# RMS pre-norms moved from the inputs of the weight units to their outputs, with the modulation column sums at other places, in a kernel of two transformer stacks

## The reference

```
for layer in range(2):
    shift, scale, gate = split(c @ mod_w[layer, 0] + mod_b[layer, 0], 3)
    h = rms_norm(x, norm_w[layer, 0, 0]) * (1 + scale) + shift
    y = mixer_ab(h) if layer == 0 else mixer_cd(h)     # attention mixers
    x = x + gate * rms_norm(y, norm_w[layer, 0, 1])
    shift, scale, gate = split(c @ mod_w[layer, 1] + mod_b[layer, 1], 3)
    h = rms_norm(x, norm_w[layer, 1, 0]) * (1 + scale) + shift
    y = (silu(h @ Wg) * (h @ Wu)) @ Wd                 # 2816 hidden
    x = x + gate * rms_norm(y, norm_w[layer, 1, 1])
# second stack: same form with shift, scale and gate from c_2 @ w_ada,
# x = x + gate * y (no norm of y), a mixer of block attention and a token
# MLP, an FFN with a 3-tap convolution over the tokens of h @ w_up, and a
# last rms_norm
```

## Time and profile before

| | us |
|---|---|
| median of 3 runs | 1102.88 |
| lowest, highest | 1096.81, 1103.98 |
| profiled execution | 1099.16 |
| its span, first to last instruction | 1097.4 |
| TensorE busy | 1040.6 (95%) |
| VectorE busy | 759.1 (69%) |
| ScalarE busy | 520.1 (47%) |

### The profile page before, as it was taken

One profiled execution on the slowest core, in us unless ns is written; L12 is line 12 of the kernel. 1 busy time (PEld: TensorE's weight loads), 2 busy tenths in 40 slices (PEclk: granted clock), 3 DMA queues, 4 the chain that ended last, 5 costly groups with the idle time before them and its releaser, 6 DMA issues.

```text
span 1097.4 us, 21157 instructions
## 1 busy us (share of the span) xinstructions
PE 1040.6 (95%) x8292; PEld 997.8 (91%) x8292; DVE 759.1 (69%) x1161; ACT 520.1 (47%) x906; POOL 4.6 (0%) x14
## 2 busy tenths in 40 slices
PE   5999879999999999999999999999977999999995
PEld 5998669999999999889999999999956999999995
DVE  3757875777777656685577777766764577777785
ACT  2445763544444455464454444446532355555552
POOL 0100000000000000000000000000000000000000
PEclk9999999999999999999999999999965999999999
DMA  9966664488888728604198898854520525545651
GB/s 353 321 208 229 237 215 171 153 307 308 313 294 307 256 74 300 199 1 137 64 315 297 307 299 307 287 211 146 181 96 1 170 85 211 186 172 185 224 186 39
DMA packets 62837, 229.12 MB, mean 209 GB/s; under 512 B 7058, under 2 KB 7314, under 8 KB 62388
## 3 DMA queue, kind: packets, MB, share of 16 engines
q1 hardware_dynamic: 61988, 225.59, 59.1%
q0 software_dynamic: 640, 2.10, 0.8%
q10 hardware_dynamic: 144, 0.52, 0.1%
HBM read 226.62 MB, written 1.57 MB: 208 GB/s over the span
## 4 chain that ended last, share of the span: by engine, by line
PE 81%; DVE 9%; ACT 5%; issue 2%; DMA 2%; SPq 0%; DVEq 0%; ACTq 0%
PE bank L1647 21%; PE bank L1649 21%; PE bank L1648 21%; PE bank L1673 3%; PE bank L1664 2%; DVE acc L549 2%; PE bank L1665 2%; DVE otok L1132 2%; ACT wH L726 1%; PE bank L1777 1%; PE bank L2273 1%; DVE hL L1127 1%; DVE wL L1080 1%; DMA modbuf<-in_mod_w 1%; PE bank L1747 1%
## 5 line engine op out<-in xcount | busy, mean ns | idle before, releaser
L1647 PE MATMUL bank<-hH,wH 128*128 128x256 f32 x1576 | 453.5, 288 | 6.5 <-DVE hL L1127 2.6
L1648 PE MATMUL bank<-hL,wH 128*128 128x256 f32 x1576 | 446.8, 284 | 0.0
L1649 PE MATMUL bank<-hH,wL 128*128 128x256 f32 x1576 | 446.7, 283 | 0.0
L1080 DVE TENSOR_TENSOR wL<-raw,wH 128x1024 fp32r<-128x1024 f32 x273 | 325.9, 1221 | 132.8 <-ACT wH L726 132.7
L1647 PEld LDWEIGHTS bank<-hH,wH 128*128 128x128 f32 x1576 | 303.2, 192 | 13.8 <-issue 8.3
L726 ACT ACTIVATE wH<-raw 128x1024 fp32r<-128x1024 f32 x273 | 273.4, 1049 | 78.1 <-PE bank L1649 59.1
L1648 PEld LDWEIGHTS bank<-hL,wH 128*128 128x128 f32 x1576 | 303.5, 193 | 0.1
L1649 PEld LDWEIGHTS bank<-hH,wL 128*128 128x128 f32 x1576 | 303.2, 192 | 0.0
L1647 PE MATMUL bank<-aH,wH 128*128 128x256 f32 x560 | 160.3, 286 | 2.1 <-DVE aL L1265 2.1
L1648 PE MATMUL bank<-aL,wH 128*128 128x256 f32 x560 | 159.7, 285 | 0.0
L1649 PE MATMUL bank<-aH,wL 128*128 128x256 f32 x560 | 159.6, 285 | 0.0
(11 more groups left out here) (295 smaller groups left out, 1123.2 us busy)
## 6 DMA issues: line engine op xcount, KB each, us to landing
raw<-in_weights SPq DMA_DIRECT2D x273, 512.0 KB, 4.9
modbuf<-in_mod_w SPq DMA_DIRECT2D x83, 512.0 KB, 5.1
modbuf<-in_w_ada SPq DMA_DIRECT2D x48, 512.0 KB, 5.2
strips<-bias_table POOLq DMA_DIRECT2D x8, 256.0 KB, 6.2
otok<-in_cmp_w SPq DMA_DIRECT2D x4, 512.0 KB, 8.6
raw<-in_mod_w SPq DMA_DIRECT2D x2, 512.0 KB, 4.9
otok<-in_mod_w SPq DMA_DIRECT2D x2, 512.0 KB, 11.3
sn<-in_mod_w SPq DMA_DIRECT2D x2, 512.0 KB, 12.8
```

The costliest lines, as they stand in the source:

```text
L1080: V.tensor_tensor(wL[:, slot, :], raw[:, slot, :], wH[:, slot, :].bitcast(F32), ALU.subtract).then_inc(lo_ready[c], 1)
L1647: mm(out, lhs_h, rhs_h, start=start, stop=False, skip_group_check=True)
L1648: mm(out, lhs_h, rhs_l, start=False, stop=False, skip_group_check=True)
L1649: return mm(out, lhs_l, rhs_h, start=False, stop=stop, skip_group_check=True)
```

## The change

1. For norms A1 to A5 the rows that go into the units are x*(1+scale)*w, without 1/rms (`raw_high` on ScalarE, `raw_low` on VectorE). hH and hL are two columns wider (HW = 258); the two hold the shift. All matmuls of projections and gate/up stream 258 columns. Behind a unit ScalarE copies the shift's column out of PSUM (`unit_column`, or `fcol` in an FFN), VectorE multiplies the 256 columns by rstd (`take_unit`, or in the FFN step), and ScalarE adds the column as bias. The sum of the squares of x is made inside and behind the first pair of units.
2. Gate and up have banks of their own (4 or 5, and 7 or 6).
3. In f0 and f1 a step's jobs stand among the chain: one behind the scaling, one behind the product. In f2 the low part of the second unit, and both parts of the third, stand inside the chain, and the 8 jobs of f2 are made in sb's output part instead. SP's order of an FFN is as before.
4. Column sums stand inside the phases: A1's before ab's last unit, A2's and A4's before the last down of f0 and f1, A3's and A5's behind the attention of cd and sb, the last gate's before f2's last down.
5. The three units that nothing reads are gone.

The diff, cut to its core:

```diff
+HW = S + 2
-AB_UNITS, CD_UNITS, SB_UNITS = 24, 27, 24
+AB_UNITS, CD_UNITS, SB_UNITS = 24, 26, 22
...
+        MOD_COLUMNS = {"modA1": ((1, 0, 16),), "modG0": ((0, 16, 24),), "modA2": ((2, 0, 16),), "modG1": ((1, 16, 24),),
+                       "modA3": ((3, 8, 16), (2, 16, 24)), "modS3": ((3, 0, 8),), "modA4": ((4, 0, 16),),
+                       "modG3": ((3, 16, 24),), "modA5": ((5, 0, 16), (4, 16, 24)), "modG5": ((5, 16, 24),)}
...
+        def gu_banks(phase, t):
+            return (bank[0] if phase == "f0" and t == 0 else bank[4 + t % 2]), bank[7 - t % 2]
...
@@ sync, phase sb
-                jobs_upto(JOBS_END["f1"] + min(KT, e // 2))
+                jobs_upto(JOBS_END["f1"] + min(KT, e // 2) + (min(KT, 2 * (e - 13)) if e >= 16 else 0))
@@ scalar
+            def raw_high(a, k):
+                act.wait_ge(x_ready, KT * (a - 1) + k + 1)
+                nc.scalar.activation(hH[:, k, 0:S], x[:, k, :], ACT.Copy, scale=sc1[:, a, k:k + 1]).then_inc(hH_ready, 1)
...
+            def raw_a(a, base):
+                n = NORMS.index(f"A{a}")
+                shift_high(a)
+                act.wait_ge(sq_used, 4 * n)
+                for b in range(4):
+                    raw_high(a, 2 * b)
+                    raw_high(a, 2 * b + 1)
+                    raw_square(a, b)
+                split_upto(base + RING)
+                norm_rstd(n)
...
+            def unit_column(phase, e, scale=1.0):
+                wait_unit(act, BASE[phase] + e)
+                nc.scalar.activation(ucol[:, e % 2:e % 2 + 1], proj_bank(phase, e)[:, S:S + 1], ACT.Copy,
+                                     scale=scale).then_inc(ucol_ready, 1)
+                act.wait_ge(ucol_ready, SCALED0[phase] + e + 1)
+                act.wait_ge(unit_scaled, SCALED0[phase] + e + 1)
...
@@ scalar, step of an FFN
-                    for c in range(2):
-                        if split:
-                            split_high(b + c, i)
-                    act.wait_ge(unit_used[1], at((base + 3 * t + 1) // 3 + 1, 2))
+                    if split:
+                        split_high(b, i)
+                        split_high(b + 1, i)
+                    up_class, up_count = cls(base + 3 * t + 1)
+                    act.wait_ge(unit_used[up_class], at(up_count, 2))
+                    for n, bk in enumerate(gu_banks(phase, t)):
+                        last = nc.scalar.activation(fcol[:, t % 2, n:n + 1], bk[:, S:S + 1], ACT.Copy)
+                    last.then_inc(col_ready, 1)
...
+                        act.wait_ge(gu_scaled, at(g0 + t + 1, 2))
                         for n in range(2):
+                            z = sq[:, t % 2, n * S:(n + 1) * S]
+                            last = nc.scalar.activation(z, z, ACT.Identity, bias=fcol[:, t % 2, n:n + 1])
+                        last.then_inc(z_ready, 1)
+                        act.wait_ge(z_ready, at(t + 1, 2))
...
                         last.then_inc(zc_ready, 1)
+                        if split:
+                            split_high(b + 2, i)
@@ vector
+            def norm_b(i, m, a, late, base):
...
                 scaled(0)
                 scaled(1)
+                mod_take(late)
                 for b in range(4):
+                    dve.wait_ge(chain.sem, done[b])
                     for k in range(2 * b, 2 * b + 2):
+                        V.scalar_tensor_tensor(out=x[:, k, :], in0=tt[:, k, :], scalar=gw1[:, m, k:k + 1],
+                                               in1=x[:, k, :], op0=ALU.mult, op1=ALU.add).then_inc(x_ready, 1)
+                    if b == 0:
+                        shift_low(a)
+                    if b < 2:
+                        scaled(b + 2)
+                    raw_low(a, 2 * b)
+                    raw_low(a, 2 * b + 1)
+                split_upto(base + RING)
...
@@ vector, step of an FFN; f2's own order is told above
+                    dve.wait_ge(col_ready, at(g0 + t + 1, 2))
+                    if phase != "f2":
+                        V.tensor_tensor(sn[:, t % 2, 0:S], gate_bank[:, 0:S], rstd[:, :], ALU.mult).then_inc(g_scaled, 1)
+                        V.tensor_tensor(pr[:, t % 2, 0:S], up_bank[:, 0:S], rstd[:, :], ALU.mult).then_inc(gu_scaled, 1)
+                        job(0, t, i)
+                        dve.wait_ge(gu_scaled, at(g0 + t + 1, 2))
+                        dve.wait_ge(silu_ready, at(g0 + t + 1, 2))
+                        V.scalar_tensor_tensor(out=sn[:, t % 2, S:2 * S], in0=pr[:, t % 2, 0:S],
+                                               scalar=fcol[:, t % 2, 1:2], in1=sn[:, t % 2, 0:S],
+                                               op0=ALU.add, op1=ALU.mult).then_inc(af_ready, 1)
+                        job(1, t, i)
...
                     dve.wait_ge(aH_ready, at(g0 + t + 1, 2))
                     V.tensor_tensor(aL[:, t % 2, :], sn[:, t % 2, S:2 * S], aH[:, t % 2, :].bitcast(F32),
                                     ALU.subtract).then_inc(aL_ready, 1)
-                    if split:
+                    if split and phase != "f2":
                         split_low(b + 2, i)
-                    if i is None:
-                        jobs_upto(lo.job + jobs_of(phase, t))
...
@@ vector, end of sb
+            split_upto(base + 19)
+            mod_take("modA5")
+            shift_low(5)
+            for b in range(4):
+                split_upto(base + 19 + 2 * b if b < 3 else end + 5)
+                jobs_upto(min(JOBS_END["sb"] + 3 * b + 3, JOBS_END["f2"]))
+                residual("sb", 4, b)
+                for k in {0: (0, 1), 1: (2, 3), 3: (4, 5, 6, 7)}.get(b, ()):
+                    raw_low(5, k)
@@ tensor
             def project(phase, e):
-                    pe.wait_ge(proj_done, PROJ0[phase] + e - 1)
+                    pe.wait_ge(unit_scaled, SCALED0[phase] + e - 1)
...
+            def first_pair(p0, outs, a, width):
...
+                    if a >= 1 and k in (3, 5):
+                        sum_square(n, (k - 3) // 2)
+                if a >= 1:
+                    sum_square(n, 2)
+                    sum_square(n, 3)
...
+                mod_sum({"f0": "modA2", "f1": "modA4", "f2": "modG5"}[phase])
                 down(FT - 1)
...
             norm_sums("B0")
-            gate_sum(0, "mod0g")
-            pe.wait_ge(mod_used, JOBS_END["ab"])
-            norm_sums_with("A1", 1, 0)
+            mod_sum("modG0")
+            keep_clock(bank[1], 6)
             ffn("f0", 1)
```

More of the change, by code:

```diff
@@ new lines, in norm_b, with residual @@
+                    if b == 0:
[5 more added lines that the diff above has]
+                split_upto(base + RING)
+            def residual(phase, m, b):
+                wait_y(dve, phase, b)
+                for k in range(2 * b, 2 * b + 2):
+                    V.scalar_tensor_tensor(out=x[:, k, :], in0=bank[b][:, (k % 2) * S:(k % 2 + 1) * S],
+                                           scalar=gw1[:, m, k:k + 1], in1=x[:, k, :],
+                                           op0=ALU.mult, op1=ALU.add).then_inc(x_ready, 1)
@@ new lines, in take_unit @@
+            def take_unit(phase, e, scale=1.0):
+                tiles, first = VALUES[phase]
+                dve.wait_ge(ucol_ready, SCALED0[phase] + e + 1)
+                if e == 0:
+                    dve.wait_ge(rstd_ready, NORMS.index("A2" if phase == "cd" else "A4") + 1)
+                if e in tiles and e - tiles[0] >= 2:
+                    dve.wait_ge(v_turned, first + e - tiles[0] - 1)
+                dst, src = unit_tile(phase, e), proj_bank(phase, e)[:, 0:S]
+                if scale == 1.0:
+                    ins = V.tensor_tensor(dst, src, rstd[:, :], ALU.mult)
+                else:
+                    ins = V.scalar_tensor_tensor(out=dst, in0=src, scalar=scale, in1=rstd[:, :], op0=ALU.mult, op1=ALU.mult)
+                ins.then_inc(unit_scaled, 1)
@@ L1506, in _ @@
             V.tensor_copy(otok[:, 1, 512:1024], bank[3][:, :]).then_inc(otok_ready, 1)
+            mod_take("modA3")
             oT_low(0)
-            for e in range(18, 27):
-                split_upto(min(base + e + 5, end + 3))
-            norm_b(2, 2)
-            norm_a(3)
+            split_upto(end + 5)
+            norm_b(2, 2, 3, "modS3", BASE["f1"])
             ffn("f1", 3)
-            norm_b(3, 3)
-            norm_a(4)
+            mod_take("modA4")
+            norm_b(3, 3, 4, "modG3", BASE["sb"])
             base = BASE["sb"]
@@ L1627, in _ @@
             mix_low(3)
-            for e in range(14, 24):
-                split_upto(min(base + e + 5, end + 3))
-            residual("sb", 4)
-            norm_a(5)
-            ffn("f2", None)
-            residual("f2", 5)
+            split_upto(base + 19)
+            mod_take("modA5")
[6 more added lines that the diff above has]
+                    raw_low(5, k)
+            split_upto(end + RING)
+            ffn("f2", 5)
+            mod_take("modG5")
+            for b in range(4):
+                residual("f2", 5, b)
             norm_a(6)
```

(23 more changed lines are left out.)

466 lines of the change are left out of this document (258 added, 208 removed).

## The result

The changed kernel takes 1182.86 us (median of 4 runs, 1179.02 to 1187.29); the kernel before beside it takes 1101.74. The ratio is 1.074, 95% interval 1.069 to 1.080: slower, as forecast, but by 81 us and not by 41, and outside the range of 1104 to 1162. Measured a second time on another occasion it took 1174.28, ratio 1.068 (1.063 to 1.072). The profiled execution took 1180.2, its span is 1178.4, 81.0 more than before.

What follows compares the result with a forecast made beforehand. TensorE's path was taken as the bound. f0 +20.5, f1 +20.5, f2 +9.3, cd +4.1, sb +3.2, its tail +1, seams -12.9, end -4.3 gave +41.4 on 1099.16: 1141 us, range 1104 to 1162.

Steps and rivals of the forecast that it cites:

- main term: f0 and f1: job 0 waits for its load, issued only after the previous step's third low part; +20.5 us each.
- L = 9.5: f0 and f1: time from job 0 to the next step's job 0, in us, against 8.68 that PE needs.
- The seams: Four transitions between phases: starting units before the sum of squares is done saves 12.9 us together, after moved column sums.
- E+8.3: Seams: first h, for the first product, ready 8.3 us after y ends at E.
- E+18.3: Seams: first pair and sum of squares end 18.3 us after y ends; gate_up(1) can start, 5.2 saved each.
- Case (c): Rival for f0 and f1: job's load lands in 5.1, L = 10.2, +34.5 each, total 1169; chance 0.13.
- Case (a): Rival for f0 and f1: load lands in 3.4, no ring closes, +4.5 each, total 1109; chance 0.18.
- C = 8.9: f2: step in us set by a ScalarE and VectorE chain, against PE's 8.68; f2 +9.3, bounds +5 and +15.
- cd and sb: Projection and attention phases: column sums behind attention, longer unit latency and wider matmuls cost +4.1 and +3.2.
- sb's tail: sb's output part: f2's jobs and their loads cause one stall of 5.7 at the last unit; net +1, bounds -4 and +4.
- The end: After the last y: squares made as y comes, last sum ends 3.5 behind it; -4.3, bounds -5 and -2.
- case (d): Rival: clock falls in the seams' idle stretches, some 2 us each, total 1149; chance 0.02.

Runs made afterwards that it cites:

- The edit: Changed kernel, but in cd and sb VectorE scales a unit before making the next low part, not behind it; 1167.9 us, ratio 1.062.
- k4_f2_order: Changed kernel, but in f2 ScalarE makes the high part of the next tile's second unit behind the copy of the two columns; 1175.4 us, ratio 1.068.
- k7_tail_f2: As k4_f2_order, but f2's eight jobs are made in f2 as in the kernel before, not in sb's output part; 1168.5 us, ratio 1.061.
- k1_sp_order: Changed kernel, but SP issues the two job loads of a step of f0 and f1 ahead of the third unit's load; 1116.1 us, ratio 1.016.
- k3_short_loads: Changed kernel, but in f0 and f1 the first and second units' loads bring 256 of 1024 columns; 1164.3 us, ratio 1.058.

## Why the prediction was right, and where it failed

The direction was right, and so was the mechanism of the main term, a ring that the load of a job closes. The size was not: +41.4 was forecast and +81.0 came. The step that failed is the sum for that ring, L = 9.5, which was closed over job 0 alone, with a landing and an issue time taken from where the loop had ended. The steps were 10.5 apart in the loop and 10.2 in the mean of all, and f0 and f1 grew by 67.8 and not 41. Point by point:

- **The seams.** E+8.3 and E+18.3 came out to the tenth in A1 and A3 (18.3 and 18.1 in all traces of the new order). The clock held there, as assumed. A2 and A4 are 1.2 longer than worked out, since the squares of y start late behind an FFN.
- **The ring of f0 and f1** exists, and it is the main term: cut on SP, it gives back 29 of 33 us in f0 and 31 of 35 in f1, on DVE 25 and 27. What was missing in L is the ring over job 1: its load is issued 1.2 behind the weight's and lands 6.1 later, which closes a ring of 10.2 by itself. That this is enough is shown by the changed kernel measured again: job 0's load landed in 4.2, as the forecast had it, and the steps were still 10.3 apart. Two other parts were short as well. Job 0's landing was put at 4.3 and had a median of 4.9 in the first trace. SP's way from the weight's load to the job's was put at 0.37, and is 0.58 (285.33 to 285.91). Both rows came from 379.8 on, the end of f0, where fewer jobs are made; inside the loop of the kernel before the first of two job loads had a median of 4.9 and the second 5.4.
- **Case (c)**, L = 10.2 and 34.5 for each FFN, had the size right (32.9 and 34.9) and got 0.13. In part that was luck: its reason was a landing of 5.1 for job 0's load, which was 4.9 in one trace and 4.2 in the other with the same f0. I had set it aside because the next tile's loads would be in already. They are not: SP issues them 2.1 behind the third unit's (287.40), while the job's is still on its way. At case (c)'s value the forecast would have been 1169. f0 and f1 make 26.8 of the 39.6 by which the span was missed, f2 6.3, A4 with sb 6.4, A2 with cd 3.2; ab came out 2.8 better.
- **Case (a)**, no ring, is refuted by the waits; its size was right, since f0 without a ring is 188.1, 3.5 above before, against 4.5 forecast. There the Trainium skill, "DMA: Bandwidth & Descriptors", "Anatomy of one DMA — SWDGE (gpsimd) path", gave 3.2 for 512 KB. The trace has 3.4 for the weight's load that goes out first, and 5.1 and 6.1 for the two jobs' loads 0.6 and 1.2 behind it: the estimate from the fit is within 0.2 us for the load that goes out first, and the ring hangs on the ones behind.
- **f2** was forecast at C = 8.9; it is 9.3 in the loop's 15 steps and 8.8 in the last ones. The step that failed is the chain on ScalarE and DVE up to the product. Counted from the copy of the columns, the bias ends at 2.1 as forecast, but the scaling on ScalarE at 3.4 and not 3.1 (a wait of 0.24 before it, and 1.09 for the pair), and with it the convolution (5.4 for 5.1), the third low part (6.5 for 6.2), the product, aH (7.5 for 7.05) and the next columns come later. A second ring over DVE's low part of nearly one length was not seen. The stretch of 15.6 is just above its bounds of 5 and 15; 1.5 of it is the clock in the last down, below.
- **cd and sb** were forecast at +4.1 and +3.2 less 3.0 each. Nothing in the forecast asked whether the chain of a unit closes a ring, as it does in sb: 3.55 a unit against 3.30 before. The edit gives 2 to 3 back there. For cd the forecast was +1.1; the two traces have +4.3 and +0.7, and the median of the nine with an unedited cd is +4.2. Of that some 1.2 is the seam of A2. The rest stays open.
- **sb's tail** was forecast at one stall of 5.7 and a net of +1: 5.26, and the stretch from the output's first product to the end of the first pair grew from 45.3 to 46.6. But the forecast saw only 0.7 to be saved there. The version without jobs takes 33.9 (853.33 to 887.18), so the jobs and their loads ate some 12 us (46.6 less 33.9 is 12.7; from k4_f2_order to k7_tail_f2, on one chip, 12.1), in two stalls and a lower clock, that the moved norm would have saved. I had counted the seam's gain as nothing where it was merely eaten.
- **The end** saved 4.3, as forecast: y ended at 1167.8, and the sums 3.5 behind it.
- **The clock**, case (d), got 0.02 with the argument that the last down ran at full pace behind a wait of 2.09. The last down of the changed kernel shows that this can't be relied on. Behind a wait of 2.28 its 24 matmuls took 4.4 us and not 2.94:

```profile
1163.40:1167.80 4.40, 4.39 (x24) 4.40 (x25) 2.77 (x7) 1.97 (x3) 0.00 (x0) 0.61 0.00 0
```

In k1_sp_order and k3_short_loads they took 2.95 at a granted clock of 1.00, behind the same wait of 2.28. Here it costs 1.5 us, and why the clock fell in one run and not in the other is not shown.

The range of 1104 to 1162 left case (c) out, by a choice of chances and not by a bound of any term. With case (c) for f0 and f1 and the upper bounds of f2 (+5.7) and sb's tail (+3) the forecast's own terms give 1178. The bounds of f0, f1, f2 and sb pointed the same way: each of them is a chain over several engines with a wait or a ring that was put down as too short, and the range was added up as if they were apart.
